# An encoder step's attention: probabilities turned by a product with a diagonal, outputs made as features by tokens

## The reference

```python
_, sel = lax.top_k(index_score, topk)
k_sel = gather(k_all, sel).astype(f32)
v_sel = gather(v_all, sel).astype(f32)
logits = jnp.einsum('bqgrd,bqkgd->bqgrk', qg, k_sel) * (hd ** -0.5)
logits = jnp.where(valid[:, :, None, None, :], logits, -jnp.inf)
p = jax.nn.softmax(logits, axis=-1)
o = jnp.einsum('bqgrk,bqkgd->bqgrd', p, v_sel)
```

## Time and profile before

| | us |
|---|---|
| median of 3 runs | 974.95 |
| lowest, highest | 973.42, 975.07 |
| the profiled execution | 973.52 |
| its span, first to last instruction | 971.8 |
| TensorE drawn busy in it | 954.7 (98%) |
| VectorE, ScalarE, GpSimd busy | 617.0, 476.0, 180.6 |
| granted TensorE clock | 0.999 of full |

### The profile page before, as it was taken

The page is one execution under the profiler, slowest core; times in us unless marked ns, Lnnn a source line. Parts: engine busy times, 40 slices in busy tenths (PEclk is TensorE's granted clock), DMA queues, the critical chain, the costliest instruction groups (busy, mean ns, idle before and its releaser), DMA issues.

```text
span 971.8 us, 17122 instructions
## 1 busy us (share of the span) xinstructions
PE 954.7 (98%) x6550; PEld 904.8 (93%) x6550; DVE 617.0 (63%) x996; ACT 476.0 (49%) x800; POOL 180.6 (19%) x301
## 2 busy tenths in 40 slices
PE   8999999999999999999999999999999999999997
PEld 6999998889999999999998899999999999788885
DVE  6278868745354368924455679688888889723214
ACT  6356436777322256421124558566666667522112
POOL 3104423323122111101001146211111112100000
PEclk9999999999999999999999999999999999999999
DMA  6812121112376467766346352234443344412313
GB/s 169 205 45 87 44 88 45 45 45 71 119 246 216 139 212 265 267 234 230 123 135 242 128 173 87 77 120 128 150 121 119 119 126 133 146 37 82 140 66 119
DMA packets 121835, 129.75 MB, mean 134 GB/s; under 512 B 14867, under 2 KB 103811, under 8 KB 119474
## 3 DMA queue, kind: packets, MB, share of 16 engines
q1 hardware_dynamic: 115330, 105.97, 34.6%
q0 software_dynamic: 6448, 22.99, 6.6%
HBM read 105.84 MB, written 23.11 MB: 133 GB/s over the span
## 4 chain that ended last, share of the span: by engine, by line
PE 90%; DVE 4%; ACT 3%; issue 2%; DMA 0%; POOL 0%; SPq 0%; ACTq 0%; DVEq 0%; POOLq 0%
PE ps L2074 11%; PE ps L2076 11%; PE ps L2075 11%; PE ps L2439 7%; PE ps L2441 7%; PE ps L2440 7%; PE ps L2083 7%; PE ps L2085 6%; PE ps L2084 6%; PE ps L2279 2%; PE ps L2093 1%; PE ps L2094 1%; PE ps L2416 1%; PE ps L2414 1%; PE ps L2415 1%
## 5 line engine op out<-in xcount | busy, mean ns | idle before, releaser
L2074 PE MATMUL ps<-xs,whi 128*128 128x288 f32 x608 | 183.4, 302 | 0.0
L2076 PE MATMUL ps<-xs,wlo 128*128 128x288 f32 x608 | 179.2, 295 | 0.0
L2075 PE MATMUL ps<-xs,whi 128*128 128x288 f32 x608 | 179.1, 295 | 0.0
L1528 DVE TENSOR_TENSOR wlo<-raw,whi 128x2048 fp32r<-128x2048 f32 (+2 forms) x36 | 78.9, 2192 | 107.6 <-ACT whi L957 107.6
L957 ACT ACTIVATE whi<-raw 128x2048 fp32r<-128x2048 f32 (+2 forms) x47 | 86.1, 1832 | 98.1 <-PE ps L2085 76.1
L2074 PEld LDWEIGHTS ps<-xs,whi 128*128 128x128 f32 x608 | 114.2, 188 | 0.7
L2075 PEld LDWEIGHTS ps<-xs,whi 128*128 128x128 f32 x608 | 114.2, 188 | 0.4
L2076 PEld LDWEIGHTS ps<-xs,wlo 128*128 128x128 f32 x608 | 114.0, 188 | 0.0
L2083 PE MATMUL ps<-whi,xs 128*128 128x256 f32 (+2 forms) x224 | 72.7, 325 | 0.1
L2085 PE MATMUL ps<-wlo,xs 128*128 128x256 f32 (+2 forms) x224 | 71.2, 318 | 0.0
L2084 PE MATMUL ps<-whi,xs 128*128 128x256 f32 (+2 forms) x224 | 71.2, 318 | 0.0
(11 more groups left out here) (370 smaller groups left out, 2615.9 us busy)
## 6 DMA issues: line engine op xcount, KB each, us to landing
raw<-in_w_in SPq DMA_DIRECT2D x21, 1024.0 KB, 6.1
raw<-in_w_down SPq DMA_DIRECT2D x10, 1024.0 KB, 4.9
saved<-in_w_up SPq DMA_DIRECT2D x36, 256.0 KB, 4.1
sums_scratch<-saved SPq DMA_DIRECT2D x9, 1024.0 KB, 4.9
raw<-sums_scratch SPq DMA_DIRECT2D x9, 1024.0 KB, 4.9
qraw<-in_w_up SPq DMA_DIRECT2D x27, 256.0 KB, 2.9
raw<-in_w_up SPq DMA_DIRECT2D x13, 512.0 KB, 3.9
raw<-in_w_up SPq DMA_DIRECT2D x26, 256.0 KB, 4.4
```

Source lines behind the costliest of these rows:

```text
L1528: nc.vector.tensor_tensor(wlo[:, p % 2, 0:n], raw[:, p % 2, 0:n], whi[:, p % 2, 0:n].bitcast(F32), ALU.subtract).then_inc(lo_ready, 1)
L2074: pe.matmul(out, wh[:, k, c0:c0 + P], xh[:, k, t], start=(k == 0), stop=False)
L2075: pe.matmul(out, wh[:, k, c0:c0 + P], xl[:, k, t], start=False, stop=False)
L2076: ins = pe.matmul(out, wl[:, k, c0:c0 + P], xh[:, k, t], start=False, stop=(k == kn - 1))
```

## The change

The turn becomes a product. VectorE, one step after a head's exponentials, takes the reciprocal of the row sums and multiplies the identity by it (`diag`, 128x128, two buffers). TensorE then multiplies the probabilities (stationary) by this diagonal (moving) instead of transposing them: they come out turned and already divided by their sum. It waits for the diagonal (`diag_ready`) instead of the exponentials. For tile 0 only the 64 real rows take part in it.

The product with the values changes sides: 64 value columns of the head's own value head are stationary, the turned probabilities move. It writes features by tokens, 64 partitions, so the transposes of the outputs, `otok`, ScalarE's copies and the wait of the logits for them are gone. VectorE copies each head's output straight into `aqt`.

`ATT_ROOM` falls from 1800 to 1300, so the top-k rounds are dealt thinner and reach on to slot 47. All who waited for five turned tiles now wait for 40 heads.

```diff
-ATT_ROOM = 1800
+ATT_ROOM = 1300
...
-        otok = at("otok", [P, QH * HD], F32, o3 + 16128)
+        diag = at("diag", [P, 2, P], F32, o3 + 16128)
...
             def saved_load(k):
                 if k == 0:
-                    sp.wait_ge(o_ready, len(ATT_TILES))
+                    sp.wait_ge(o_ready, NATT)
...
                         if n == 0:
-                            pool.wait_ge(o_ready, len(ATT_TILES))
+                            pool.wait_ge(o_ready, NATT)
...
                         if tt == 0:
-                            nc.scalar.activation(pt[:, m % 2, 0:P], ps[:, 6, 0:P], ACT.Copy)
-                            ins = nc.scalar.activation(pt[0:DEC, m % 2, P:2 * P], ps[0:DEC, 6, P:2 * P], ACT.Copy)
+                            nc.scalar.activation(pt[:, m % 2, 0:DEC], ps[:, 6, 0:DEC], ACT.Copy)
+                            ins = nc.scalar.activation(pt[0:DEC, m % 2, P:P + DEC], ps[0:DEC, 6, P:P + DEC], ACT.Copy)
...
-                    m = n - 4
-                    if m >= 0 and m % QH == QH - 1:
-                        t = m // QH
-                        tt = ATT_TILES[t]
-                        act.wait_ge(o_turned, t + 1)
-                        k = rows(tt)
-                        nc.scalar.activation(aqt[:, :, tok(tt).start:tok(tt).start + k],
-                                             ps[:, 4 + (n + 1) % 2, :].rearrange("p (b c) -> p b c", b=4)[:, :, 0:k], ACT.Copy).then_inc(o_ready, 1)
...
+                    m = n - 1
+                    if 0 <= m < NATT:
+                        dve.wait_ge(probs_ready, m + 1)
+                        link(nc.vector.reciprocal(rinv[:, m % 2:m % 2 + 1], rowsum[:, m % 4:m % 4 + 1]))
+                        if m >= 2:
+                            dve.wait_ge(probs_turned, m - 1)
+                        nc.vector.tensor_scalar(diag[:, m % 2, :], ident[:, :], rinv[:, m % 2:m % 2 + 1], None, ALU.mult)\
+                            .then_inc(diag_ready, 1)
                     m = n - 3
                     if 0 <= m < NATT:
-                        h = m % QH
-                        dve.wait_ge(probs_ready, m + 1)
-                        link(nc.vector.reciprocal(rinv[:, m % 2:m % 2 + 1], rowsum[:, m % 4:m % 4 + 1]))
+                        tt, h = ATT_TILES[m // QH], m % QH
+                        k, half = rows(tt), slice(64 * (h % 2), 64 * (h % 2) + 64)
                         dve.wait_ge(pv_done, m + 1)
-                        if m >= QH and h == 0:
-                            dve.wait_ge(o_turned, m // QH)
-                        g = h // (QH // KVH)
-                        nc.vector.tensor_scalar(otok[:, HD * h:HD * h + HD], ps[:, 7, HD * g:HD * g + HD],
-                                                rinv[:, m % 2:m % 2 + 1], None, ALU.mult).then_inc(o_scaled, 1)
+                        nc.vector.tensor_copy(aqt[half, h // 2, tok(tt).start:tok(tt).start + k], ps[0:HD, 7, 0:k]).then_inc(o_ready, 1)
...
                         if n >= 2:
                             pe.wait_ge(masked, n - 1)
-                        if n >= 12 and (n - 5) % QH == QH - 1:
-                            pe.wait_ge(o_ready, (n - 5) // QH + 1)
...
                     if 0 <= m < NATT:
-                        pe.wait_ge(probs_ready, m + 1)
+                        tt = ATT_TILES[m // QH]
+                        q = rows(tt)
+                        pe.wait_ge(diag_ready, m + 1)
                         if m >= 1:
                             pe.wait_ge(pt_ready, m)
-                        for i, (c, k) in enumerate(key_blocks(ATT_TILES[m // QH])):
-                            ins = pe.transpose(ps[0:k, 6, P * i:P * i + P], lg[:, m % 3, c:c + k], ident[:, :])
+                        for i, (c, k) in enumerate(key_blocks(tt)):
+                            ins = pe.matmul(ps[0:k, 6, P * i:P * i + q], lg[0:q, m % 3, c:c + k], diag[0:q, m % 2, 0:q],
+                                            start=True, stop=True)
                         ins.then_inc(probs_turned, 1)
...
                         if m >= 1:
-                            pe.wait_ge(o_scaled, m)
+                            pe.wait_ge(o_ready, m)
                         blocks = key_blocks(tt)
+                        q, g = rows(tt), m % QH // (QH // KVH)
+                        v = slice(HD * g, HD * g + HD)
...
-                            ins = pe.matmul(ps[:, 7, 0:128], pt[0:k, m % 2, P * i:P * i + P], val,
+                            ins = pe.matmul(ps[0:HD, 7, 0:q], val[:, v], pt[0:k, m % 2, P * i:P * i + q],
                                             start=(i == 0), stop=(i == len(blocks) - 1))
                         ins.then_inc(pv_done, 1)
-                    m = n - 4
-                    if m >= 0 and m % QH == QH - 1:
-
-                        pe.wait_ge(o_scaled, m + 1)
-                        for b in range(4):
-                            ins = pe.transpose(ps[:, 4 + (n + 1) % 2, P * b:P * b + P], otok[:, P * b:P * b + P], ident[:, :])
-                        ins.then_inc(o_turned, 1)
```

More of the change, by code:

```diff
@@ L449, in layer_kernel @@
         logits_done, masked, probs_ready = sem("logits_done"), sem("masked"), sem("probs_ready")
-        probs_turned, pt_ready, pv_done, o_scaled = sem("probs_turned"), sem("pt_ready"), sem("pv_done"), sem("o_scaled")
-        o_turned, o_ready = sem("o_turned"), sem("o_ready")
+        probs_turned, pt_ready, pv_done, o_ready = sem("probs_turned"), sem("pt_ready"), sem("pv_done"), sem("o_ready")
+        diag_ready = sem("diag_ready")
         soft_ready, diff_ready = sem("soft_ready"), sem("diff_ready")
@@ L2295, in aux @@
                             pe.wait_ge(decay_used, 3 * GH)
-                            pe.wait_ge(o_ready, len(ATT_TILES))
+                            pe.wait_ge(o_ready, NATT)
                         else:
```

## The result

The changed kernel takes **990.12 us** (989.56 to 991.06, 4 runs), the kernel before on the same chip 974.6 us (973.42 to 975.07, 4 runs). The ratio is 1.0163, with an interval of 1.0150 to 1.0176; between the medians 15.5 us are lost. The forecast was 982.0 us with a range of 975 to 988. The sign was right. The size was not, and the time lies outside the range. The profiled execution took 990.17 us for a span of 988.5 us, 16.7 us longer than the span before.

What follows compares the result with a forecast made beforehand. TensorE, busy in 98% of the span, was taken as the bound. Its own work +8.0 us (turn +9.2, sample heads +1.0, outputs -2.2) and stalls +6.5 - 7.4 gave +7.1 on 974.95: 982.0 us, range 975 to 988.

Steps and rivals of the forecast that it cites:

- The values of whole tiles: Values product on TensorE: halving the weights to 64 columns saves 0, bounds 0 and -9 us.
- rival (c): Values product: narrow weights switch the array's mode twice per head, +11.5 us over 32 heads, 993.5 us; chance 0.10.
- The stalls: TensorE's attention waits: walking VectorE's queue step by step gave 6.5 us after against 7.4 us before, changing places.
- The turn: Whole-tile probabilities: 80 blocks turned by f32 product at 0.224 instead of 0.109 us each, +9.2 us.
- Rival (e): Turn: a transpose is four times faster than an ordinary product, not two; 999 us, chance 0.02.
- Sample heads: Eight heads with 64-row turn: changed rows and cheaper values, +0.14 us a head, +1.0 us; bounds -1 and +3 us.
- Outputs: TensorE: 20 transposes of outputs go, at 0.109 us each, -2.2 us.
- VectorE's diagonal: VectorE: making the 128-column diagonal takes 0.2 us per step, bounds 0.15 and 0.3 us.
- The spread of top-k: VectorE: nine rounds move behind slot 36, ending at slot 47, relieving it up to 175 us and loading 183 to 218 us.
- Rival (d): Values product: records fall to half, 9 us go, 973.1 us with the forecast's waits; chance 0.07 for faster.
- (b): Attention's waits: the thinner top-k spread removes them all, +0.6 us, 975.5 us; chance 0.15.
- (f): VectorE falls behind for good, another 4 us of waits, 986 us and a little more; chance 0.06.

Runs made afterwards that it cites:

- Run 6: Kernel before plus one unused transpose of 64 columns between turn and values product of each of 40 heads; 978.89 us.
- run 5: Kernel before plus one unused f32 product with 64 weight columns between turn and values product of each of 40 heads; 990.33 us.
- run 1: Changed kernel with all 128 value columns stationary, VectorE copying the head's 64 partitions; 984.9 us, ratio 1.0113.
- Run 3: Changed kernel with ATT_ROOM set back from 1300 to 1800; 989.65 us, ratio 1.0162.
- run 4: Kernel before with only ATT_ROOM lowered from 1800 to 1300; 977.28 us, ratio 1.0032.
- run 12: Kernel before with top-k dealt more densely, ATT_ROOM 2200 instead of 1800; 972.86 us, ratio 0.9981.
- run 7: Changed kernel with transposed turn, 128 value columns and VectorE dividing the exponentials in place, ATT_ROOM 1300; 976.95 us, ratio 1.0030.
- run 8: Changed kernel with transposed turn, 128 value columns and VectorE dividing the exponentials in place, ATT_ROOM 1800; 976.13 us, ratio 1.0016.
- run 10: Changed kernel turned by transposes that wait for the exponentials, diagonal made but unread, division left out; 981.81 us, ratio 1.0075.
- run 11: Kernel before with ScalarE's copy of the turned outputs placed ahead of the step's exponentials; 974.98 us, ratio 1.0006.
- run 2: Changed kernel turned by transposes, diagonal still made and waited for, division left out; 982.85 us, ratio 1.0085.
- run 9: Changed kernel with 128 value columns and the sample heads' turn contracting over all 128 rows; 985.7 us, ratio 1.0115.

## Why the prediction was wrong

**The values of whole tiles: the step that failed.** The prediction set them at 0 with bounds of 0 and -9 us, and kept the cost of a change of mode as rival (c), with a chance of 0.10. Measured are 0.36 us a head in tile 1 and 0.31 to 0.33 us in tiles 2 to 4, over the 32 heads **+10.5 us**. The mechanism was thought of and its price was right (0.36 us, worked out from the change of rows). The evidence against it was not evidence: the piece of the earlier trace rows without a gap was a transpose with 64 columns. Run 6 repeats it and finds no gap, run 5 does the same with a product and finds 0.34 us. The term's own bounds were drawn from how long one record is held, and not from what lies between two of different widths, so their upper end was 0 where a known neighbour (rows) cost 0.1 us. The records between two changes did stay 0.11 us apart, as forecast, but for the first, which is followed after 0.16 us: together (0.87 - 0.28)/5 = 0.118 us for the six of a tile 3 head.

**The stalls: the second step that failed, the other way.** Forecast 6.5 us, measured 2.5 + 3 x 0.16 = 3.0 us by the same counting. The walk itself holds: run 1 is the kernel that it described, with narrow weights free, and its waits come to 5.6 + 6 x 0.16 = 6.6 us. The two longest stand where the walk put 1.4 us (step 21) and 2.55 us (step 29):

```profile
174.40 0.71 PE L2261 MATMUL ps<-diag,lg 128*128 128x128 f32 x4 [1.21 <-DVE diag L1664]
...
213.69 0.94 PE L2261 MATMUL ps<-diag,lg 128*128 128x128 f32 x6 [2.22 <-DVE diag L1664]
```

In the changed kernel the same stalls are shorter, since TensorE comes later to each of them:

```profile
175.74 0.71 PE L2260 MATMUL ps<-diag,lg 128*128 128x128 f32 x4 [0.89 <-DVE diag L1664]
...
214.77 0.94 PE L2260 MATMUL ps<-diag,lg 128*128 128x128 f32 x6 [1.29 <-DVE diag L1664]
```

So a wrong term of TensorE's own work also made the waits wrong, with the opposite sign. Rival (c), which kept 6.5 us of stalls, gave 993.5 us; with the 3.0 us it gives 990.0 us. That this meets the measured time is partly luck: its 11.5 us are 1.0 us too many, and its sample heads 1.2 us too few.

**The counting of stalls leaves some out.** A stall shorter than what a matmul is drawn too long shows no idle time and stands in no list of waits. Step 24 of the changed kernel, the diagonal and the turn:

```profile
189.21 0.29 DVE L1664 TENSOR_SCALAR diag<-ident,small 128x128 f32<-128x128 f32 x1
189.25 0.34 PE L2250 MATMUL ps<-k_lo,q_split 128*128 128x384 f32 x1
189.56 0.71 PE L2260 MATMUL ps<-diag,lg 128*128 128x128 f32 x4
```

The turn starts 0.06 us behind the diagonal's end, as it does in steps 21, 25 and 29, and 0.31 us behind the logits instead of 0.17 us; the next record follows 0.1 us later than usual. Steps 19 and 26 are the same, and step 23 has a short stall too. Counted in this way, from start to start against steps without a stall, all stalls are 4.4 us in the changed kernel, 8.0 us in the kernel before and 7.7 us in run 1.

**The turn: right.** 192 records, 0.112 us apart in whole tiles ((0.83 - 0.28)/5 us for six), +9.2 us. Rival (e), a factor of four, is out.

**Sample heads: undersized.** Forecast +0.14 us a head, +1.0 us; measured +0.27 us, +2.2 us, inside the bounds. The head of step 14, in the changed kernel:

```profile
145.45 0.28 PE L2250 MATMUL ps<-k_lo,q_split 128*128 128x192 f32 x1
145.65 0.69 PE L2260 MATMUL ps<-diag,lg 64*128 64x64 f32 x4
146.27 0.33 PE L2277 MATMUL ps<-pt,cache 128*64 128x64 f32 x2
146.53 0.32 PE L2277 MATMUL ps<-pt,v_low 64*64 64x64 f32 x2
146.78 0.39 PE L2088 MATMUL ps<-whi,xs 128*128 128x256 f32 x1
```

From the logits to the values it is 0.82 us. Before, the same stretch is 0.33 us, so the turn costs 0.49 us more and not 0.25 us. The step priced the changes of rows and overlooked that the four records are of two widths, 128 and 64 columns, so a change of columns lies within the turn as well. From the values to the next slot it is 0.51 instead of 0.73 us, a gain of 0.22 us where 0.11 us were forecast.

**Outputs: right.** -2.2 us on TensorE.

**VectorE's diagonal: undersized.** Forecast 0.2 us with 0.3 as the upper bound; its median is 0.286 us, its mean 0.396 us (15.8 us over 40) and its longest 1.2 us:

```profile
L1664 DVE TENSOR_SCALAR diag<-ident,small x40: 285/286/1199, 91.2 to 274.7; 128x128 f32<-128x128 f32 x40
```

The line through 256 and 512 columns of the earlier trace rows doesn't reach down to 128. What that costs in the changed kernel wasn't measured: six of its turns start right behind a diagonal (above), so it isn't nothing by this record.

**The spread of top-k: neutral as taken.** Run 3 finds no difference. Alone it is a loss of 3 us (run 4), which the prediction didn't price, and the gain lies in the other direction (run 12).

**The sum, with the measured terms.** 9.2 (turn) + 10.5 (width) + 2.2 (sample heads) - 2.2 (outputs) + 4.4 - 8.0 (stalls, from start to start) + 0.4 (both executions differ by that before attention begins) = 16.5 of the 16.7 us between the spans. The prediction's own tests decided correctly: attention's stretch is 16.2 us longer and not 5 to 9, so it said itself that it was wrong.

**Rival (d)**, the values' records at half, isn't seen: they stay 0.11 us apart with 64 weight columns. **Rivals (b) and (f)** weren't reached, since the work on TensorE grew by 19.7 us and not by the 8.0 us that both assume.

## What to carry to other kernels

Look at every border between matmuls of different shape, rows and columns, and price it apart from the records; a border that costs nothing between transposes says nothing of products. Keep narrow products together, or widen them: 128 columns cost the same 0.11 us a record as 64 here and save 0.34 us a head. Where an engine is full but has waits, work taken off it comes back as waits and work added fills them, so a term of its own work moves the time by less than its size (run 5: 16.2 us for 22.4, run 1: 5.2 for 10.5 less 1.7); first find whose queue is late (here VectorE's, in runs 7, 8, 10 and 11), and move work out of its way, as run 12 does for 1.5 us. Read stalls from start to start where matmuls are drawn over each other.

## What the runs showed of the hardware

**A narrow f32 product, 64 columns among 128, costs 0.34 us for the change of width there and back; a narrow transpose in the same place costs none** (runs 5 and 6).

**A stall of about 2 us can cost another 1.5 us behind it, by the clock.** The kernel before and run 12 have the same 2.31 us of idle at step 28. The stretches behind it, of the kernel before and then of run 12 (columns as in the earlier trace rows; the third number from the right is the granted clock):

```profile
202.00:204.00 2.00, 1.51 (x12) 1.50 (x13) 1.93 (x3) 1.32 (x3) 0.00 (x0) 1.00 1.04 357
204.00:206.00 2.00, 2.00 (x19) 2.00 (x19) 1.97 (x5) 0.00 (x0) 0.00 (x0) 1.00 0.24 86
```

```profile
200.00:202.00 2.00, 1.58 (x11) 1.58 (x12) 1.93 (x3) 1.24 (x3) 0.00 (x0) 0.87 1.06 362
202.00:204.00 2.00, 2.00 (x11) 2.00 (x11) 1.97 (x5) 0.00 (x1) 0.00 (x0) 0.50 0.24 85
204.00:206.00 2.00, 2.00 (x15) 2.00 (x15) 0.32 (x2) 1.97 (x6) 0.00 (x0) 0.78 0.02 4
```

In run 12's profiled execution the granted clock falls to 0.50, 1.2 instead of 2.4 GHz, after the stall, and 11 records pass in 2 us instead of 19; step 28 takes 5.83 us instead of 4.30 us, 1.5 us more. That execution has a mean clock of 0.997; the two shortest runs of the ten (971.04 and 971.49 us) have 0.999 and 0.998. The same fall stands behind the longest stall in the profiled executions of runs 2, 4, 6, 7, 8, 9 and 10, and behind another one in those of runs 7 (1.92 us), 8 (1.94 us) and 11 (1.86 us, in step 21):

```profile
172.00:174.00 2.00, 2.00 (x12) 2.00 (x11) 1.90 (x8) 1.30 (x3) 0.00 (x0) 0.50 0.03 8
```

So it followed stalls of 1.86 to 3.46 us and failed to follow others of up to 2.31 us. A fall cost 1.3 to 1.7 us, and in step 29 of run 7, with the longest time at 0.50, about 2.4 us. In runs 7 and 8 the fall in step 29 (about 2.4 and 1.5 us) is half of what their spans are above that of the kernel before (5.1 and 2.9 us). It explains two more results. In run 4 step 28 takes 5.86 us, so 1.6 of its 3 us are the clock and the rest is the longer wait. In run 9 it takes back what the sample heads gained (from step 29 to step 30 it loses 4.42 us against the kernel before, run 1 only 2.82 us, at the same wait of 2.22 us). In run 1 and in the changed kernel the clock stays at 1.00, so the comparison that decides the main question is free of it. The other executions have no trace; the mean clock of those of the kernel before is 0.995 to 0.999, so they may hold such falls too. Why it falls in some and not in others wasn't tried.

**The in-place division on VectorE** took 0.46 to 0.49 us in the mean at each of five widths from 128 to 512 columns (run 7). Its shortest rise with the width, from 0.285 us at 128 to 0.486 us at 512, where all eight lie within 0.486 and 0.490 us; at the smaller widths single ones took up to 1.4 us, and what stretches those wasn't separated.
